# A two-layer streaming encoder step: the recurrence's projections and operands in one stage, the first tile's expert choice beside the second tile's chunks

## The chip, the cores and the metric

The kernel runs on one core of a Trainium2 chip. The number that counts is the time on the device in microseconds (us), as the median of three runs of the whole program. All data are float32. The engines are named PE (TensorE, matrix products), DVE (VectorE), ACT (ScalarE), POOL (GpSimd) and SP (SyncE, which only issues DMAs here).

## What is computed

384 tokens of width 1024 go through two layers: 256 of a prompt and 8 streams of 16 samples. Layer 0 mixes with an RWKV-7 recurrence, layer 1 with differential attention. Behind each mixer stands a PEER layer, which chooses 16 of 16384 experts per head (8 heads) and token:

```python
r, k, v = xr @ w_rkv[0], xk @ w_rkv[1], xv @ w_rkv[2]      # x* = x + (x_prev - x) * mu[i]
decay = exp(-exp(-softplus(-(w0 + tanh(xw @ w1) @ w2)) - 0.5)); a = sigmoid(a0 + (xa @ a1) @ a2)
S = S * d - (S kk)(kk * a)^T + v k^T;  y = S r             # token by token, 16 heads of 64
out = ((group_norm(y) + bonus) * g) @ w_out
x = layer_norm(ALPHA * x + out)
q = x @ w_query;  s = q . sub_keys                         # 2 x 128 scores a head
experts, gate = top 16 of the 16 x 16 sums of the best of each half, softmax
x = layer_norm(ALPHA * x + sum_k gate_k * gelu(u[e_k] . x) * v[e_k])
```

Each token and layer needs 128 rows of `u` and as many of `v`, 4 KB each. The kernel finds `u` and `v` of an expert side by side (8 KB).

## The kernel before

The tokens are three tiles of 128: tiles 0 and 1 are the prompt, tile 2 the samples. A stage is one block of the program with its own queues for each engine, and all engines meet at its end.

**Front part, one stage after the other.** `rwkv_projections` (L182) makes r, k, v, the decay's argument z, a and g of all three tiles and stores them in DRAM (`spill`). Then for tile 0 and again for tile 1: `wkv_operands` (L366; products of r, k, a with decays and their inverses), `wkv_chunks` (L465; the recurrence inside chunks of 16 tokens, 16 heads in groups of four), `wkv_states` (L787; the chunks' states in series) and `wkv_outputs` (L889; norm, own term, gate). Both tiles together: `load_rows` (L876), `to_features` (L939), `project_and_norm` (L990). After `mixing_weight` (L2342) and one more `to_features`, `open_flow` (L1523) makes the queries of both tiles and the scores and the choice of tile 0, and issues the first gathers.

**The flow.** `Flow` (L1175) spreads the experts' work over the stages that follow. One gather (`DMA_INDIRECT`, L1361) brings the `u` and `v` rows of one slot for 128 partitions, 1.05 MB; it is called a pair here, and there are 768, 128 for each tile and layer. A pair lands in one of 8 or 10 places of SBUF (`fl_pairs`, 8, and `fl_more`, 2 that are not there for the pairs in `NARROW`). DVE makes the dots with `u` (L1287), ACT the gelu (L1313) and the diagonal matrices (L1307), PE the sums with `v` (L1334), after which the place is free for the next gather. Two pairs are a unit, so there are 384. Each stage calls `flow.plan(ticks, last)` (L1224): it has `ticks` points at which a bit of the flow's work stands in each engine's queue, and `last` is the unit whose dots are due at its end. `turn_rows_out` and `turn_rows_in` (L1365, L1371) send a finished choice through DRAM into the order of the gathers. `Choice` (L1095) is the top-16 search on DVE, in small steps that also go into ticks.

**Beside the flow.** `mixing_tile` (L2963) does tile 2 of layer 0: for each half of the heads `half_operands` (L2393), `half_chunks` (L2510, 8 heads in groups of two, 35 ticks) and `half_outputs` (L2833), then the projection (`project_tile`, L2239) and the scores (`key_scores`). `attention_tile` (L3003) does layer 1 of a tile, three times. `run_flow` and `ffn_norm` end the program. Weights come in pieces of 1 MB through a ring of four places (`Pieces`, L1390, `pc_ring`).

Engines take their instructions in order; each queue waits by itself. POOL's queue holds the gathers, the products that spread operands over chunks (L776, L2816) and a few stores; SP's holds the weights' loads.

## Time and profile before

| | before |
|---|---|
| median of 3 runs | 3212.89 us (3206.84 to 3549.92) |
| span of the profiled execution | 3201.7 us |
| PE, PE weight loads | 66%, 35% busy |
| DVE, ACT, POOL | 56%, 21%, 33% busy |
| DMA | 1019.44 MB, mean 318 GB/s |
| HBM | 992.71 MB read, 18.39 MB written |

The profile is one execution. Its page cuts the span in 40 slices, 80 us each, with a digit for the busy share in tenths; further views give groups of instructions, waits, DMA issues and stretches. A stretch is written start:end in us from the span's start. In a group's line, x is the number of instructions, then busy us and the mean ns of one, then the engine's idle time before them and what ended most of it. The shares above are means over parts with different limits.

### The profile page before, as it was taken

The numbers are of one execution on the slowest core, as the hardware profiler recorded it, in microseconds if no ns is written. First come the engines' busy times: TensorE is split into PE (matmuls) and PEld (weight loads), VectorE is DVE, ScalarE is ACT, GpSimd is POOL, SyncE is SP. The second block draws the span as 40 slices with busy tenths as digits, with TensorE's granted clock in tenths as the row PEclk, the third lists the DMA queues.
The fourth block names the chain that finished last, engine by engine and source line by source line (L and its number), as shares of the span: only waits on it lengthen the run. The fifth ranks groups of instructions, "written<-read, shape, count | busy, mean of one in ns | idle before, by whom it ended". The sixth has DMA issues, their size and how long they took to land. (4 is left out here: it accounts for less than half of the span.)

```text
span 3201.7 us, 31542 instructions
## 1 busy us (share of the span) xinstructions
PE 2122.0 (66%) x10729; PEld 1110.6 (35%) x10729; DVE 1808.7 (56%) x4190; ACT 675.9 (21%) x1920; POOL 1060.0 (33%) x990
## 2 busy tenths in 40 slices
PE   6949668482577586758567585576767758655555
PEld 3427456270144253423224232234223434322222
DVE  2044454227786675576665765756744454965555
ACT  1012121010221321211431112511213221121111
POOL 0003122003356463334333333433333223454442
PEclk9979789795689797879788787788878878878877
DMA  5230200344889999999999999899999999999998
GB/s 173 92 138 1 78 3 18 110 130 199 346 324 369 372 389 408 420 404 403 408 371 420 399 397 416 345 413 420 383 412 405 420 401 410 360 383 421 420 420 335
DMA packets 152814, 1019.44 MB, mean 318 GB/s; under 512 B 17872, under 2 KB 18944, under 8 KB 37456
## 3 DMA queue, kind: packets, MB, share of 16 engines
q0 software_dynamic: 117024, 825.84, 64.2%
q1 hardware_dynamic: 35632, 191.58, 15.4%
q8 instruction: 88, 1.44, 0.2%
q14 instruction: 70, 0.57, 0.0%
HBM read 992.71 MB, written 18.39 MB: 316 GB/s over the span
## 5 line engine op out<-in xcount | busy, mean ns | idle before, releaser
L1334 PE MATMUL fl_acc<-fl_pairs,fl_diag 128*64 128x512 f32 x2576 | 820.8, 740 | 462.9 <-ACT fl_diag L1307 431.8
L1361 POOL DMA_INDIRECT fl_pairs<-in_peer_uv,fl_row_at x644 | 733.4, 1139 | 1116.0 <-PE fl_acc L1334 999.7
L1287 DVE CUSTOM_DVE_ANT_0 fl_pairs<-fl_pairs,fl_rows 128x1024 f32<-128x1024 f32 x644 | 789.5, 1245 | 398.3 <-DMA fl_pairs<-in_peer_uv,fl_row_at 396.9
L1334 PEld LDWEIGHTS fl_acc<-fl_pairs,fl_diag 128*64 128x64 f32 x2576 | 281.8, 162 | 879.4 <-issue 816.3
L1313 ACT ACTIVATE fl_acts<-fl_dots 128x2 f32<-128x2 f32 x384 | 78.0, 203 | 1247.6 <-DVE fl_dots L1287 1247.1
L1307 ACT ACTIVATE fl_diag<-constants_sb,fl_mix 128x64 f32<-128x64 f32 x768 | 224.2, 341 | 323.6 <-DVE fl_mix L1277 320.1
L1334 PE MATMUL fl_acc<-fl_more,fl_diag 128*64 128x512 f32 x496 | 171.7, 790 | 132.3 <-ACT fl_diag L1307 115.9
L1361 POOL DMA_INDIRECT fl_more<-in_peer_uv,fl_row_at x124 | 143.0, 1153 | 266.8 <-PE fl_acc L1334 245.9
L1287 DVE CUSTOM_DVE_ANT_0 fl_more<-fl_more,fl_rows 128x1024 f32<-128x1024 f32 x124 | 150.0, 1223 | 118.5 <-DMA fl_more<-in_peer_uv,fl_row_at 118.0
L1792 PE MATMUL aacc<-pc_ring,at_xT 128*128 128x512 f32 x288 | 139.8, 629 | 16.0 <-PEq L1719 16.0
L1334 PEld LDWEIGHTS fl_acc<-fl_more,fl_diag 128*64 128x64 f32 x496 | 60.1, 168 | 214.7 <-issue 206.0
L284 PE MATMUL acc<-w_ring,mixed 128*128 128x512 f32 x288 | 126.0, 599 | 10.0 <-issue 9.1
L1277 DVE TENSOR_TENSOR fl_mix<-fl_row_gate,fl_acts 128x2 f32<-128x2 f32 x384 | 68.8, 181 | 110.4 <-ACT fl_acts L1313 62.6
L1484 PEld LDWEIGHTS lbank_late<-at_yT,pc_ring 128*128 128x128 f32 x768 | 90.8, 197 | 25.3 <-issue 25.3
L1484 PE MATMUL lbank_late<-at_yT,pc_ring 128*128 128x128 f32 x768 | 95.9, 284 | 4.3 <-PEq L1719 4.3
L348 DVE SCALAR_TENSOR_TENSOR mixed<-dxT,mu_cols,xT 128x384 f32<-128x384 f32 x48 | 25.8, 612 | 114.5 <-PEq L293 114.5
L1792 PEld LDWEIGHTS aacc<-pc_ring,at_xT 128*128 128x128 f32 x288 | 54.1, 198 | 100.8 <-issue 100.8
L284 PEld LDWEIGHTS acc<-w_ring,mixed 128*128 128x128 f32 x288 | 55.1, 192 | 80.2 <-issue 80.2
L1579 PE MATMUL obank<-peer_xT,fl_pairs 128*128 128x256 f32 x256 | 58.2, 389 | 12.4 <-DMA fl_pairs<-in_query_by_head 12.4
L721 DVE TENSOR_TENSOR x<-bank,x 128x512 f32<-128x512 f32 x32 | 22.1, 692 | 75.1 <-PE bank L579 75.1
L1287 DVE DVE_READ_ACCUMULATOR2_ANT fl_dots<- 128x1 f32 x768 | 63.1, 82 | 0.0
L2052 PE MATMUL sa_b<-pc_ring,sa_pT 128*32 128x128 f32 x512 | 53.3, 299 | 13.8 <-ACT sa_pT L2082 13.8
(510 smaller groups left out, 2828.0 us busy)
## 6 DMA issues: line engine op xcount, KB each, us to landing
pc_ring<-in_kvq_by_pair SPq DMA_DIRECT2D x36, 1024.0 KB, 9.3
pc_ring<-in_query_by_head SPq DMA_DIRECT2D x32, 1024.0 KB, 9.8
pc_ring<-in_past_k SPq DMA_DIRECT2D x16, 1024.0 KB, 12.0
pc_ring<-in_past_v SPq DMA_DIRECT2D x16, 1024.0 KB, 11.2
w_ring<-in_rwkv_w_rkv SPq DMA_DIRECT2D x24, 512.0 KB, 3.6
pc_ring<-in_out_by_pair SPq DMA_DIRECT2D x12, 1024.0 KB, 9.8
fl_pairs<-in_peer_uv,fl_row_at POOLq DMA_INDIRECT x644, 16.3
fl_pairs<-in_query_by_head SPq DMA_DIRECT2D x8, 1024.0 KB, 11.0
```

What stands on the lines that cost most here:

```text
L284: mm = pe.matmul(acc[:, 2 * t + h, :], xm[:, k, t * P:(t + 1) * P], w_ring[:, n % RING, h * HALF:(h + 1) * HALF], start=(k == 0), stop=(k ...
L348: ins = dve.scalar_tensor_tensor(mixed[:, j % 2, k, :], dxT[:, k, :], mu_cols[:, i * KD + k:i * KD + k + 1], xT[:, k, 0:TOK], ALU.mult, AL ...
L1277: dve.tensor_tensor(self.mix[:, u % 2, q, :], self.row_gate[:, u % TILES, :, q], self.acts[:, u % 2, q, :], ALU.mult).then_inc(*self.mix_d ...
L1287: dve.tensor_tensor_reduce(pair, pair, self.rows[:, u % 2, j, :], 1.0, 0.0, ALU.mult, ALU.add, self.dots[:, u % 2, q, j:j + 1]).then_inc(* ...
L1307: act.activation(self.diag[:, self.diagged % self.DIAGS, j, :], self.core.const("fold_ident"), ACT.Copy, scale=self.mix[:, u % 2, q, j:j + ...
L1313: act.activation(self.acts[:, u % 2, q, :], self.dots[:, u % 2, q, :], ACT.Gelu).then_inc(*self.gelu_done.by())
L1334: mm = pe.matmul(self.acc[j * FOLD:(j + 1) * FOLD, half, :], self.diag[:, self.summed % self.DIAGS, j, :], self.pair(g)[:, D + half * HALF ...
L1361: pool.indirect_dma_start(self.pair(g), None, self.io["peer_uv"], bass.IndirectOffsetOnAxis(ap=self.row_at[:, u % TILES, j, q:q + 1], axis ...
L1484: mm = pe.matmul(self.bank[m % 3][:, 0:P], w[:, k, (m % 2) * P:(m % 2 + 1) * P], self.xT[:, k, :], start=(k == 0), stop=(k == KD - 1))
L1579: mm = pe.matmul(bank[m % 3][:, 0:WIDTH], wq[:, m // 2 % RING, k, (m % 2) * P:(m % 2 + 1) * P], xT[:, k, :], start=(k == 0), stop=(k == KD ...
L1792: mm = pe.matmul(acc[:, 2 * i + h, :], xT[:, k, :], pieces.tile(first + n // 2)[:, n % 2 * D + h * HALF:n % 2 * D + (h + 1) * HALF], start ...
L2052: mm = pe.matmul(o_bank[rows, g * P:(g + 1) * P], pT[:, g, j, rows], v, start=(j == 0), stop=(j == KT), tile_position=(0, h * HR))
```

## The change

**One stage for projections and operands.** `rwkv_operands` takes the place of `rwkv_projections` and of the operands' stages (`wkv_operands`, and `half_operands` for tile 2). The order of the six projections is now w, a, r, k, v, g, tile by tile within r, k, v, with the sums of the logs of the decay between them (`log_sums`). DVE makes the operands of a tile in two steps (`keys`, `decayed`), with one buffer for `e_incl`, `e_end`, `B`, `B_end`, `K_end` that the tiles share. POOL stores eight operands a tile in DRAM (`operands`, 4.2 MB a tile), and the own term and the gate (`gates`). Later stages load them into an `Operands` buffer.

**Order.** Then come `wkv_chunks` and `wkv_states` of tile 0. `Flow` and its accumulator are opened, and `half_chunks` runs over all 16 heads of tile 1 (`WideTile`, in groups of two: 63 ticks) with `FirstTile` in its ticks: outputs, projection, norm, queries, scores and choice of tile 0, with a ring of its own of two places for the 12 pieces of weights. Its gathers begin at the end of that stage. The ring of pairs is opened then (`open_ring`), and tile 1's states and outputs (`half_outputs`) follow, in which no pair is due before the states are done (`since`). `mixing_weight` stands after it with three ticks. `second_tile` does tile 1's projection, queries and scores beside the flow, with its own load of the same 12 pieces. Tile 1's choice moves into tile 2's chunks.

**Numbers.** `NARROW`, the pairs that have 8 places, is 0 to 195 (before 24 to 175), and all `last` numbers are new. The rest of the program is as it was.

```diff
-def rwkv_projections(core, io, buf):
...
+class Operands:
...
+    NAMES = ("a", "r", "B", "k", "v", "e_end", "B_end", "K_end")
...
+    def load(self, sp, t, parts):
+        for i, part in enumerate(parts):
+            for q in range(2):
+                sp.dma_start(self.tile[:, i, 4 * q:4 * q + 4], self.core.operands[t, :, part, 4 * q:4 * q + 4]).then_inc(*self.came[i][q].by(16))
+        self.since = [[s.last() for s in pair] for pair in self.came]
...
+def rwkv_operands(core, io):
...
+                def operands(t):
+                    for i, (n, src) in enumerate((("r", r[:, t]), ("B", B[:]), ("k", k[:, t % 2]), ("B_end", B_end[:]), ("K_end", K_end[:]), ("a", a[:, t]))):
+                        pool.wait_ge(*out_done.at(6 * t + i + 1))
+                        put(n, t, src, away[f"k{t % 2}" if n == "k" else n])
+                    put("e_end", t, e_end, away["e_end"])
...
+                lora("w")
+                lora("a")
+                project("r", 0)
+                log_sums(0, 0)
+                project("r", 1)
+                log_sums(0, 1)
+                project("r", 2)
+                project("k", 0)
+                project("k", 1)
+                log_sums(1, 0)
+                project("k", 2)
+                log_sums(1, 1)
+                project("v", 0)
+                log_sums(2, 0)
+                project("v", 1)
+                log_sums(2, 1)
+                project("v", 2)
+                lora("g")
...
+                        act.wait_ge(*away["e_end"].at(16 * t))
...
+                mix("w")
+                mix("a")
+                mix("r")
+                mix("k")
+                exclude(0, 0)
+                exclude(0, 1)
+                mix("v")
+                keys(0)
+                decayed(0)
+                exclude(1, 0)
+                keys(1)
+                exclude(1, 1)
+                mix("g")
+                decayed(1)
+                exclude(2, 0)
+                own_term(0)
+                keys(2)
+                own_term(1)
+                exclude(2, 1)
+                decayed(2)
+                own_term(2)
         core.end_stage()
...
-def wkv_operands(core, io, buf, w, t):
-def load_rows(core, io, gated, tiles):
-def wkv_outputs(core, io, buf, w, t):
-def to_features(core, src, dst, name, tiles):
-def project_and_norm(core, io, actT, weight, layer, name, tiles):
-def open_flow(core, io, flow, xT, last):
-def half_operands(core, io, flow, x, last, **events):
...
-    NARROW = range(24, 176)
+    NARROW = range(0, 196)
...
-            due = self.first + (self.last - self.first) * n // self.ticks
+            due = self.first + (self.last - self.first) * max(0, n - since) // (self.ticks - since)
...
+    def open_ring(self, ctx):
+        def sb(name, shape):
+            return ctx.enter_context(self.core.nc.sbuf_tensor("fl_" + name, shape, F32, side="right"))
+        self.ring, self.rows = sb("pairs", [P, self.KEPT, 2 * D]), sb("rows", [P, 2, GROUPS, D])
...
-    flow.plan(TICKS, last, lags=flow.LOOSE, **events)
+    beside.plan(TICKS, last, lags=Flow.LOOSE, **events)
...
+class FirstTile:
...
+    PLACES = 2
+    PIECES = KD // 2 + PH
...
+        for i in range(self.PIECES):
+            if i == self.PLACES:
+                sp.wait_ge(*self.vec_free.at(1))
+                sp.dma_start(self.vec[:, 0], io["ln_mix_g"][0:1, :].broadcast_to([P, D])).then_inc(*self.vec_in.by(16))
+                sp.dma_start(self.vec[:, 1], io["ln_mix_b"][0:1, :].broadcast_to([P, D])).then_inc(*self.vec_in.by(16))
+            if i >= self.PLACES:
+                sp.wait_ge(*self.used.at(i - self.PLACES + 1))
+            sp.dma_start(self.piece(i), sources[i]).then_inc(*self.came[i % self.PLACES].by(16))
+        sp.wait_ge(*self.rows_in.at(16 * TILES))
...
+            self.flow.turn_rows_out(pool, 0)
+            self.flow.turn_rows_in(pool, 0)
...
+        n = 30
+        for q in range(4):
+            yield n
+            dve.wait_ge(*self.s_done.at(q + 1))
+            part = choice.best_of(dve, choice.scores, q)
+            for i in range(4):
+                advance(part, 6)
+                n += 1
+                if i < 3:
+                    yield n
+            drain(part)
+        part = choice.rest(dve, 0)
+        while n < self.ticks:
+            yield n
+            advance(part, 4)
+            n += 1
+        yield n
+        drain(part)
...
+        for m in range(2 * PH):
+            yield 23 + m
...
+def second_tile(core, io, flow, x, gated, ops, at):
...
+            x = HalfTile(core, of_half, t, ops)
+            for part in range(2):
...
+        rwkv_operands(core, io)
...
+                    wkv_chunks(core, Operands(core, raw, "0", 2), w, 0)
+                ops = Operands(core, first, "1", 2, side="right")
+                wkv_states(core, w, 0, lambda sp: ops.load(sp, 1, range(2)))
+            flow = Flow(core, io, ctx)
+            first_gated = ExitStack()
+            rows = first_gated.enter_context(nc.sbuf_tensor("st_gated", [P, D], F32))
+            kept = ExitStack()
+            x = WideTile(core, kept, 1, ops)
+            with ExitStack() as beside:
+                half_chunks(core, FirstTile(core, io, flow, beside, both, carry, x), x)
+        flow.open_ring(ctx)
+        half_outputs(core, io, flow, x, rows, 6, since=NCH + 2, rows=((0, 1),))
+        kept.close()
+        mixing_weight(core, io, flow, neg_lam, 7)
+        with ExitStack() as of_sample:
+            ops = Operands(core, of_sample, "2", 1, side="right")
+            second_tile(core, io, flow, x, rows, ops, [(9, {}), (17, {}), (19, {}), (33, dict(rows=((1, 1),)))])
+            first_gated.close()
...
-    pieces = mixing_tile(core, io, flow, 2, None, later, [
-        (19, dict(choose=1, side=25)), (39, dict(side=50, end=18, turn=((1, 21, 24),))), (47, {}), (52, {}), (72, {}), (80, {}), (81, {}), (87, {}), (88, {}), (100, {})])
+    pieces = mixing_tile(core, io, flow, 2, ops, of_sample, later, [
+        (56, dict(choose=1, side=175, end=12, turn=((1, 15, 18),))), (64, {}), (82, {}), (90, {}), (92, {}), (99, {}), (101, {}), (110, {})])
```

## Rows read from the trace of the kernel before

**Rows 1.** The page's 40 slices of 80 us: DMA engines' busy share in tenths.
```profile
DMA  5230200344889999999999999899999999999998
```
**Rows 2.** Stretches (start:end, length, then as the first line says).
```profile
core 0: us, PE busy (x) PEld busy (x) DVE busy (x) ACT busy (x) POOL busy (x), PEclk, DMA share, GB/s
0.00:201.00 201.00, 166.78 (x405) 74.44 (x405) 38.36 (x72) 21.95 (x37) 11.43 (x20) 0.99 0.41 137
201.00:238.70 37.70, 5.35 (x8) 2.08 (x8) 22.60 (x21) 8.81 (x9) 0.00 (x0) 0.59 0.34 125
238.70:347.30 108.60, 95.76 (x656) 72.31 (x656) 44.31 (x89) 26.70 (x56) 42.61 (x45) 0.96 0.00 1
347.30:368.30 21.00, 19.61 (x512) 18.93 (x512) 8.40 (x19) 0.04 (x1) 0.00 (x0) 0.81 0.01 3
368.30:760.10 391.80, 228.13 (x1612) 173.00 (x1610) 170.35 (x392) 59.26 (x112) 50.30 (x59) 0.77 0.21 70
552.50:570.90 18.40, 2.12 (x13) 1.54 (x11) 12.31 (x13) 2.67 (x4) 0.00 (x0) 0.50 0.25 86
570.90:627.70 56.80, 33.94 (x80) 16.29 (x80) 14.05 (x22) 1.89 (x6) 0.00 (x0) 0.77 0.36 138
636.90:760.10 123.20, 65.27 (x322) 57.27 (x320) 54.30 (x210) 12.51 (x27) 7.72 (x14) 0.78 0.32 89
886.10:1005.60 119.50, 96.64 (x712) 57.69 (x712) 98.89 (x182) 31.39 (x102) 79.94 (x71) 0.93 0.86 334
1091.30:1199.80 108.50, 91.14 (x712) 55.71 (x712) 78.85 (x147) 30.58 (x104) 70.14 (x66) 0.97 0.99 388
1254.60:1391.70 137.10, 101.58 (x496) 55.75 (x496) 77.55 (x245) 26.04 (x91) 47.66 (x42) 0.85 1.01 419
1391.70:2822.70 1431.00, 968.51 (x4220) 453.87 (x4220) 890.77 (x2195) 346.91 (x1037) 503.99 (x463) 0.82 0.99 398
1005.60:3184.20 2178.60, 1446.55 (x6680) 688.00 (x6680) 1327.14 (x3120) 498.78 (x1531) 828.77 (x753) 0.82 0.99 401
```
**Rows 3.** DMA in 1005.6:3184.2: issues with KB each and median us to landing.
```profile
DMA packets 124870, 872.89 MB, mean 401 GB/s; under 512 B 14667, under 2 KB 15179, under 8 KB 21195
...
pc_ring<-in_past_k SPq DMA_DIRECT2D x16, 1024.0 KB, 12.0
...
fl_pairs<-in_peer_uv,fl_row_at POOLq DMA_INDIRECT x566, 17.0
...
fl_more<-in_peer_uv,fl_row_at POOLq DMA_INDIRECT x120, 17.3
```
**Rows 4.** Waits of DVE in 1005.6:3184.2: us in total, times, longest us.
```profile
DVE fl_pairs L1287 <- DMA fl_pairs<-in_peer_uv,fl_row_at: 369.7, 248, 4.3
```
**Rows 5.** Timeline of POOL, 744:762: start us, us, instruction, idle before and releaser.
```profile
753.15 0.59 POOL L1368 DMA_DIRECT2D turn_at<-fl_expert  x1 [110.58 <-DVEq L1172]
...
760.13 1.05 POOL L1361 DMA_INDIRECT fl_pairs<-in_peer_uv,fl_row_at  x1 [1.89 <-DMA fl_row_gate<-turn_gate]
```
**Rows 6.** The page's groups: PE's products of the projections.
```profile
L284 PE MATMUL acc<-w_ring,mixed 128*128 128x512 f32 x288 | 126.0, 599 | 10.0 <-issue 9.1
```
**Rows 7.** DMA issues over the whole span: KB each, median us to landing.
```profile
w_ring<-in_rwkv_w_rkv SPq DMA_DIRECT2D x24, 512.0 KB, 3.6
...
spill_v<-buf_v POOLq DMA_DIRECT2D x1, 1536.0 KB, 5.7
```
**Rows 8.** Groups by form, 886.1:1005.6, the first chunks' stage beside the pairs.
```profile
L1334 PE MATMUL fl_acc<-fl_pairs,fl_diag 128*64 128x512 f32 x160 | 44.3, 665 | 3.0 <-ACT fl_diag L1307 3.0
...
L2816 POOL TENSOR_TENSOR hc_B_by_chunk<-hw_B_end,constants_sb 128x512 f32<-128x512 f32 x8 | 10.4, 1304 | 0.1
```
**Rows 9.** Groups by form, 238.7:347.3, tile 0's chunks.
```profile
L776 POOL TENSOR_TENSOR v_by_chunk<-wkv_v,constants_sb 128x512 f32<-128x512 f32 x16 | 16.6, 1040 | 0.0
```
**Rows 10.** Groups by form, 1254.6:1391.7: queries of a tile and its projection.
```profile
L1484 PE MATMUL lbank_late<-mt_xT,pc_ring 128*128 128x128 f32 x256 | 32.9, 288 | 3.2 <-PEq L1719 3.2
...
L2276 PE MATMUL pt_acc<-pc_ring,mt_T 128*128 128x512 f32 x32 | 14.8, 604 | 3.2 <-PEq L1719 3.2
```

1376 lines of the change are left out of this document (669 added, 707 removed).

## Prediction

> **What bounds the kernel now.** I read the page's slices first [rows 1]. Read the DMA line: it stands at 9 from about the fifteenth slice to the end, and is low before that. So the kernel has a front part in which the DMA engines are mostly idle, and a long rest in which they are full. The table of stretches makes this exact [rows 2]: from 1005.6 us to 3184.2 us the DMA share is 0.99, at 401 GB/s, while PE is busy 1446.6 of 2178.6 us and DVE 1327.1. No compute engine is the limit there. What moves is the gathered pairs: 566 and 120 gathers of 128 rows of 8 KB, 1.049 MB each, are 719.3 MB of the 872.9 MB of this stretch [rows 3]. The waits of DVE in it agree: its longest ones are for pairs to land [rows 4]. The last 17.5 us hold the closing norm and no transfers that count.
>
> Ahead of the rest, the first gather is issued only at 760.1 us, 7.0 us after the first tile's choice is softmaxed [rows 5]. The stretch 368.3 to 760.1 runs at 70 GB/s: the second tile's operands, chunks, states and outputs, then both tiles' projection, then both tiles' queries, then the first tile's choice, one after the other. So two quantities decide the time: when the DMA engines become full, and how many bytes are left then.
>
> **The change, part by part.**
>
> *Projections and operands in one stage.* Before: 201.0 us, then 37.7 us of operands for tile 0 [rows 2], again 42 us for tile 1 (in the merged stretch), and two stages of them for tile 2 beside the pairs. After: one stage. PE keeps its 166.8 us and gets 12 sums of logs, 512 columns each, two passes apiece; the projections' row has 288 such passes in 126.0 us, 0.44 us each [rows 6], so 0.9 us for a sum and 10 us in all. DVE gets the operands of three tiles: 22.6 us each [rows 2], 68 us, beside 38.4 us it had. They hang in a chain with single buffers (`e_incl`, `e_end`, `B_end` are reused by each tile, and ACT waits for the last tile's DMA before it overwrites): a tile's keys and decays take some 21 us of DVE, then the store must land, some 6 us by the nearest row, 5.7 us for a store of 1.5 MB [rows 7], and PE's third tile waits on `log_sums`. PE's three projections take 45 us each with the sums, so the chain fits in except for two stalls of about 3 us. Then g's copies wait for the last operands, and the stage ends 6 us after the last store as before: 201 + 10 + 6 = 217 us. Bounds: 211 (no stall) and 201 + 68 = 269 (nothing hidden).
>
> *Chunks and states of tile 0.* Their code is the same: 108.6 and 21.0 us [rows 2]. The chunks now begin with loads of 1 MB pieces: PE waits for the first, some 6 us (512 KB took 3.6, 1 MB in a full queue 12.0 [rows 3, 7]). The operands' 37.7 us are gone. 217 + 114.6 + 21 = 353 us, against 368.3 before.
>
> *Tile 1's chunks (16 heads in groups of two, 63 ticks) with tile 0's outputs, projection, norm, queries and choice beside them.* This is the term that weighs most. PE: a stage of this code for 8 heads has PE busy 96.6 us, of which 44.3 are the pairs' products [rows 2, 8]; 52.3 remain, 105 for 16 heads. Beside it FirstTile has 14.8 us for the projection, 32.9 us for the queries [rows 10], and for the scores (32 passes, an eighth of the queries' 256) and the transposes some 8: 56 us. Together 161. DVE: 44.3 us for 16 heads by the nearest row, plus 12.3 us of outputs, 7 of norm (14.05 for two tiles) and 54.3 of choice [rows 2]: 118 us. In the two stages of this kind that the trace has, PE is busy 96.6/119.5 = 0.81 and 91.1/108.5 = 0.84 of the time, with DVE at 0.83 and 0.73 [rows 2]. With PE at 0.84 and less DVE I take 161/0.855 = 188 us, then 8 us for the exponent, the softmax and the turn of the rows (7.0 in [rows 5]). 353 + 196 = 549 us for the first gather, 211 us earlier. Bounds of the 188: 161 (PE never waits), and every inserted piece in series with the chain: 63 ticks at 119.5/35 = 3.4 us, 215 us, and 56 + 74 + 10 = 140 us on top, 355. The two-place ring of pieces is covered if a tick takes over about 3 us: a 1 MB piece serves two ticks and takes between 3.6 us (512 KB) and 12.0 us (1 MB, queue full) [rows 3, 7]; the queue is empty here, so I take it at the low end.
>
> GpSimd's spreading of the operands is also in this stage: 32 products and 8 diagonals. The row shows 1304 ns for one beside the pairs' two-input products on DVE, and 1040 ns in the stage without them [rows 8, 9]. The Trainium skill (GPSIMD Engine Reference, section Specifications) states that GpSimd shares its SBUF interfaces with VectorE and contends with it when DVE reads two SBUF inputs. The rows agree in direction, and the new stage puts more such DVE work beside it. At 1304 ns this is 52 us of GpSimd in a stage of 188, off the path, so both readings leave the sum where it is unless the chunks wait for it (a few us).
>
> *No pair handled until the second tile's states are done.* Gathers fill 8 places at once (8.4 MB, some 21 us), then the queue is idle. In the outputs' stage, the nearest rows are states 21.0 and outputs 18.4 us [rows 2]; six steps of dots stand among them, and the first sums come two ticks after the first dots. I take 48 us until a place comes free: full from 597 us, with 8 gathers issued. Bounds: 30 and 60.
>
> *What is left to move.* Before, 686 gathers were left at 1005.6 us [rows 3]; after, 760 are left at 597 us: 74 x 1.049 = 77.6 MB more. To this come tile 1's own 12 pieces, 12.6 MB (new: tile 1 no longer shares the projection and the queries with tile 0), tile 2's operands, 4.2 MB, against 2.1 MB of old ones, and 2.5 MB of norm vectors, rows and gates. 872.9 + 94.8 = 967.7 MB. At the 400.6 GB/s of this stretch that is 2416 us. So the change pays 31 us for the sharing given up, and this is in the sum.
>
> *The new schedule (`last` numbers) and tile 2.* Its first chunks now carry 23 units (two pairs each) instead of 20, and tile 1's whole final choice. That stage before was not full: 0.86 and 334 GB/s, DVE at 0.83 [rows 2]. With about 20 us more DVE work it would take some 140 us for 49 MB, which at 400.6 need 122: between 0 and 20 us lost, I take 10. Two operand stages are gone from there, which only takes work off engines that had time. Fewer places (8 to pair 195, not 175) cost nothing by the rows: the stretch 1091.3 to 1199.8 had 8 places and was full, 0.99 [rows 2]. The final part is as before.
>
> **Sum.** 597 + 2416 + 10 + 17.5 = 3040 us for the span, against 3201.7. The median shown, 3212.9, is 11 us over that span, so I predict 3051 us, 5.0% less. Range of this case alone: the merged stage from 161 to 230 us, the rate from 398 to 408 GB/s (398 was held over 1431 us [rows 2]): 2980 to 3115.
>
> **The rivals.**
>
> *Full rate, not average (chance 0.08).* If the new schedule keeps the queue as full as 1254.6 to 1391.7, 419 GB/s [rows 2], the rest takes 2310 us: 2945. Against it: the dips lie in attention and head norms, which are unchanged.
>
> *The merged stage turns into a chain (0.10).* PE, DVE and ACT take their queues in order, so each piece of FirstTile stands in the way of the chunk's next step. In [rows 2] that stage reaches PE 0.81 with the pairs beside it, which speaks against it; but its dots had no dependents among the chunks' neighbours, and FirstTile is itself one chain. At 260 to 355 us the time is 3123 to 3218.
>
> *Early part not full (0.08).* With 8 places and dense ticks, the part up to unit 110 (about 272 MB) could run at the 334 GB/s of 886.1 to 1005.6: 814 instead of 679 us, 3186 in all. The later stage of this kind, at 388 and 0.99 [rows 2], speaks against it. Here a rule of the skill would be harsher: DMA: Bandwidth & Descriptors, section Bandwidth, says that for transfers between HBM and SBUF the HBM side, some 358 GB/s, binds. By it the 967.7 MB would need 2703 us, and the kernel would be slower. The row shows 401 over 2178.6 us, so the measurement decides, and the rule has no part in the chance.
>
> *Slower (0.03).* The place: the merged stage's ring of two pieces. If it is a chain (355 us) and each of its 12 pieces is also waited for at 12.0 us, the longest landing row [rows 3], 144 us come on top: 499 us, 3362 in all. It decides from 415 us on: there the time passes 3277. Against it: this queue is empty while PE works, so pieces land sooner.
>
> *It does not do what it says (0.01).* If the first gather did not move, the time would be as before. Nothing in the diff suggests it; the stages that stood ahead of it are gone.
>
> **Chances.** The forecast has 0.70. A difference of 2% is about what a measurement of this kernel can tell from none, so the marks are 3149 and 3277. Faster: 0.70, plus 0.08, plus 0.07 of the chain (short of 3149) and 0.03 of the part not full: 0.88. Same: 0.03 + 0.05 + 0.01 = 0.09. Slower: 0.03. The range 2970 to 3120 holds most of the forecast's case and some of its neighbours, near 8 in 10.
>
> **What would show it.** The first gather near 549 us (before 760), the merged stage near 196 us with PE busy about 161, the first stage near 217, the DMA line at 9 from about 600 us on, some 968 MB after it at 400 GB/s. The prediction is wrong if the merged stage passes 260 us, if the DMA share between 600 and 1250 us stays under 0.9, or if the first stage is over 240 us because the reused buffers wait for their stores.

## Result, and the profile after

| | before | after |
|---|---|---|
| median | 3209.9 us | 3126.6 us (3121.8 to 3131.1) |
| ratio to before, 95% interval | | 0.976 [0.974, 0.979] |
| span of the profiled execution | 3201.7 us | 3128.9 us |
| DMA | 1019.4 MB, 318 GB/s | 1039.6 MB, 332 GB/s |
| PE, DVE busy | 66%, 56% | 69%, 57% |

The change gains 2.4%. (One run of the kernel before, 3549.9 us, was in a slower state of the chip; it stands in the median before and is left out of the ratio.) Forecast were 3051 us, 5.0%, and a range of 2970 to 3120, which the result misses by 6.6 us. The direction is as forecast, and the front part within 23 us; the gain is half the size.

The page's DMA line after the change, in 40 slices of 78 us, against [rows 1]:

```profile
DMA  3440330489979999989999999999999999889998
```

The full part begins at the ninth slice instead of the eleventh to thirteenth. But a 7 and several 8s stand in it. The table of stretches has the stages one by one (columns as in [rows 2]):

```profile
0.00:227.90 227.90, 179.22 (x429) 79.73 (x429) 96.83 (x123) 52.38 (x81) 29.34 (x48) 0.96 0.42 151
227.90:343.10 115.20, 98.63 (x656) 74.98 (x656) 43.26 (x88) 26.77 (x56) 42.69 (x45) 0.91 0.09 37
343.10:364.50 21.40, 19.53 (x512) 18.47 (x512) 8.40 (x19) 0.00 (x0) 0.00 (x0) 0.85 0.50 199
364.50:560.80 196.30, 161.44 (x1451) 132.90 (x1449) 114.04 (x322) 39.13 (x97) 46.01 (x49) 0.89 0.26 90
565.40:639.80 74.40, 37.99 (x536) 32.80 (x536) 31.61 (x47) 8.22 (x18) 14.54 (x18) 0.52 0.60 217
832.20:976.30 144.10, 107.44 (x736) 63.55 (x736) 120.77 (x240) 34.22 (x112) 82.59 (x77) 0.86 0.86 337
1035.30:1136.00 100.70, 87.91 (x655) 53.98 (x657) 71.98 (x131) 27.03 (x92) 64.34 (x60) 0.96 0.91 349
1367.10:1398.50 31.40, 12.82 (x32) 5.05 (x32) 29.04 (x55) 3.10 (x13) 5.79 (x5) 0.63 0.72 297
1814.70:1908.90 94.20, 75.57 (x200) 27.90 (x200) 53.04 (x98) 17.17 (x51) 35.67 (x32) 0.90 0.96 385
2351.40:2569.40 218.00, 155.77 (x1218) 90.76 (x1216) 104.14 (x263) 62.70 (x179) 59.98 (x56) 0.82 0.98 403
2695.20:2755.60 60.40, 30.75 (x80) 12.11 (x76) 57.46 (x131) 9.99 (x30) 23.10 (x22) 0.65 0.76 281
645.40:3111.10 2465.70, 1659.79 (x7837) 813.16 (x7833) 1488.81 (x3533) 540.36 (x1689) 940.53 (x858) 0.82 0.97 390
```

In the order of the rows: first stage; tile 0's chunks; its states; the merged stage; tile 1's states and outputs with the first gathers; tile 2's first and second chunks; the short stage with choice 2; one of the three attention projections; the sample attention; the stage of the last choice; all of it from the 13th gather on. For the like stages of the kernel before, beside [rows 2], four more rows of its table: the short stage with choice 2, attention projections, sample attention, last choice:

```profile
1420.40:1441.70 21.30, 10.15 (x29) 3.77 (x25) 16.44 (x58) 2.63 (x11) 8.71 (x8) 0.70 1.01 421
1441.70:1533.70 92.00, 72.54 (x200) 26.86 (x200) 53.19 (x98) 16.37 (x50) 38.66 (x32) 0.93 1.00 405
2748.60:2822.70 74.10, 43.11 (x120) 17.88 (x120) 68.28 (x155) 14.41 (x47) 34.58 (x32) 0.75 0.95 361
2381.80:2616.20 234.40, 156.91 (x1241) 89.92 (x1240) 111.52 (x278) 65.33 (x188) 67.61 (x62) 0.81 1.01 414
```

The fullest stretches stand at 419 to 421 GB/s, before and after. So I call *idle time* of a stretch its length times (1 - rate/420). The sample attention before: 234.4 x (1 - 414/420) = 3.3 us; the last choice after: 60.4 x (1 - 281/420) = 20.0 us. (The Trainium skill, Perfetto Trace Analysis, section Roofline, puts the ceiling of a core that works alone at its 16 DMA engines, about 435 GB/s; the rows agree with that and not with the 358 GB/s that the prediction weighed.)

The forecast's sum against the measured one, in us of span:

| term | forecast | measured | miss |
|---|---|---|---|
| first stage | 217 | 227.9 | +11 |
| tile 0's chunks and states | 136 | 136.6 | +1 |
| merged stage | 188 | 196.3 | +8 |
| to the first gather | 8 | 11.1 | +3 |
| from the first to the 13th gather | 48 + 4.2 MB at 400.6 = 58.5 | 73.5 | +15 |
| the rest | 963.5 MB at 400.6, + 10 = 2415 | 960.9 MB at 389.7: 2465.7 | +51 |
| the end | 17.5 | 17.8 | 0 |
| span | 3040 | 3128.9 | +89 |

The bytes are right within 2.6 MB (6 us), so the rate alone is 57 us too long. Its idle time is 2465.7 - 960.9/0.42 = 178 us; at 400.6 GB/s and with the 10 us it would be 121. Most of these 57 us stand in the stages above. Idle time after against the like stage before: tile 2's first chunks 28.5 against 5.6 at the average rate plus the 10 allowed (+13), its second chunks 17.0 against 8.3 (+9), the short stage 9.2 against 0 (+9), three attention projections 18.9 against 11.2 together (+8), sample attention 8.8 against 3.3 (+5), last choice 20.0 against 10.4 (+10): 54 us. These are six places picked because they lost; elsewhere gains and losses nearly cancel, such as 4 us less in the two prompt attentions and 5 us more in the norm behind the last choice.

### The profile page after: what moved, and what is told of

The parts are those of the page before. It is cut to its first block and busy times, and to the rows that moved or that the text cites. A ratio compares the mean times of both kernels' runs of the same rounds, so it can differ in the third digit from the quotient of the medians.

```text
span 3128.9 us, 33004 instructions
## 1 busy us (share of the span) xinstructions
PE 2164.7 (69%) x11433; PEld 1155.5 (37%) x11433; DVE 1792.7 (57%) x4150; ACT 672.7 (21%) x1953; POOL 1075.8 (34%) x1022
## 5 line engine op out<-in xcount | busy, mean ns | idle before, releaser
L1326 PE MATMUL fl_acc<-fl_pairs,fl_diag 128*64 128x512 f32 x2608 | 843.4, 751 | 463.4 <-ACT fl_diag L1299 431.9
L1684 PE MATMUL aacc<-pc_piece,at_xT 128*128 128x512 f32 x288 | 140.3, 632 | 12.3 <-PEq L1611 12.3
L367 PE MATMUL ro_acc<-ro_w_ring,ro_mixed 128*128 128x512 f32 x288 | 125.1, 593 | 0.5 <-PE ro_acc L367 0.5
L1479 PEld LDWEIGHTS lbank_late<-at_yT,pc_piece 128*128 128x128 f32 x768 | 91.9, 199 | 26.2 <-issue 26.2
L1479 PE MATMUL lbank_late<-at_yT,pc_piece 128*128 128x128 f32 x768 | 96.7, 285 | 4.5 <-PEq L1611 4.5
L1684 PEld LDWEIGHTS aacc<-pc_piece,at_xT 128*128 128x128 f32 x288 | 54.7, 201 | 100.0 <-issue 100.0
L367 PEld LDWEIGHTS ro_acc<-ro_w_ring,ro_mixed 128*128 128x128 f32 x288 | 54.9, 191 | 70.2 <-issue 70.2
L1944 PE MATMUL sa_b<-pc_piece,sa_pT 128*32 128x128 f32 x512 | 60.3, 324 | 26.0 <-ACT sa_pT L1974 26.0
L1944 PEld LDWEIGHTS sa_b<-pc_piece,sa_pT 128*32 128x32 f32 x512 | 53.3, 129 | 38.7 <-ACT sa_pT L1974 35.2
L1305 ACT ACT_TABLE_LOAD x47 | 60.3, 1283 | 0.8
L2168 PE MATMUL pt_acc<-pc_piece,at_oT 128*128 128x512 f32 x96 | 48.6, 644 | 8.6 <-PEq L2084 8.6
```

The source lines that it names most:

```text
L367: mm = pe.matmul(acc[:, 2 * t + h, :], mixed[:, j % 2, i, t * P:(t + 1) * P], w_ring[:, n % RING, cols[h]], start=(i == 0), stop=(i == KD ...
L1305: act.activation(self.acts[:, u % 2, q, :], self.dots[:, u % 2, q, :], ACT.Gelu).then_inc(*self.gelu_done.by())
L1326: mm = pe.matmul(self.acc[j * FOLD:(j + 1) * FOLD, half, :], self.diag[:, self.summed % self.DIAGS, j, :], self.pair(g)[:, D + half * HALF ...
L1479: mm = pe.matmul(self.bank[m % 3][:, 0:P], w[:, k, (m % 2) * P:(m % 2 + 1) * P], self.xT[:, k, :], start=(k == 0), stop=(k == KD - 1))
L1684: mm = pe.matmul(acc[:, 2 * i + h, :], xT[:, k, :], pieces.tile(first + n // 2)[:, n % 2 * D + h * HALF:n % 2 * D + (h + 1) * HALF], start ...
L1944: mm = pe.matmul(o_bank[rows, g * P:(g + 1) * P], pT[:, g, j, rows], v, start=(j == 0), stop=(j == KT), tile_position=(0, h * HR))
```

## Experiments

Times are medians, the ratio is to the kernel before with its 95% interval. A run's median can be off by a few us, so a small effect is read from the stage in which it stands. A stage also scatters: tile 2's first chunks, with the same schedule, take 141 to 144 us in the traces of nine kernels.

| run | us | ratio |
|---|---|---|
| e0_after | 3126.1 | 0.9758 [0.9741, 0.9775] |
| e1_since0 | 3115.6 | 0.9730 [0.9706, 0.9755] |
| e2_spread | 3119.4 | 0.9742 [0.9723, 0.9761] |
| e3_shift | 3137.7 | 0.9801 [0.9775, 0.9827] |
| e4_fewer_bytes | 3111.1 | 0.9712 [0.9696, 0.9729] |
| e5_two_e_end | 3111.3 | 0.9704 [0.9685, 0.9722] |
| e6_early_turn | 3149.7 | 0.9826 [0.9804, 0.9849] |
| e7_last_choice | 3119.9 | 0.9741 [0.9720, 0.9761] |
| e8_combo | 3070.8 | 0.9593 [0.9571, 0.9615] |
| e9_eight_places | 3199.5 | 0.9985 [0.9973, 0.9998] |
| e10_late_turn | 3117.3 | 0.9728 [0.9710, 0.9747] |
| e11_more_in_chunks | 3121.6 | 0.9755 [0.9729, 0.9780] |
| e12_combo_late | 3057.4 | 0.9565 [0.9531, 0.9599] |
| e13_combo_boundary | 3055.1 | 0.9558 [0.9524, 0.9592] |

**The changed kernel again (e0).**

> The changed kernel once more, beside the three runs that follow, as their common reference. Ratio to the kernel before 0.976, as recorded, within 0.003.

As expected. The others are compared with 3126 us. Below, a due number is a `last` number of the plan.

**Why the first stage takes 228 us (e5).** ACT's and PE's waits in the changed kernel's first stage (us, times, longest):

```profile
ACT L436 <- DMA operands<-ro_rows: 21.8, 1, 21.8
...
ACT ro_rows L436 <- DMA operands<-ro_rows: 13.9, 1, 13.9
```

```profile
PE ro_aux L385 <- DVE ro_z L512: 10.2, 1, 10.2
```

ACT may not write the next tile's `e_end` into the buffer from which POOL's store still reads. The edit (the first of its three places is the second buffer; that ACT writes and DVE reads them in turn is left out here):

```diff
+        e_ends = [rows[:, 2], sb("e_end2", [P, D])[:]]
...
-                        act.wait_ge(*away["e_end"].at(16 * t))
+                        if t == 2:
+                            act.wait_ge(*away["e_end0"].at(16))
```

> One buffer more for e_end in the first stage, so that ACT doesn't wait for the store of the tile before (waits of 13.9 and 21.8 us on it in the changed kernel; PE waits 10.2 us on z and 9.3 us on mixed behind them). Theory A (the stores' landing in the shared buffers is what makes this stage 227.9 us instead of the forecast 217): the stage becomes 8 to 12 us shorter, and the whole as much. Rival B (PE's waits come from DVE's queue, which does each tile's operands in order, and from the stores at the end): the stage is the same within 3 us.

The stage of e5:

```profile
0.00:210.00 210.00, 177.26 (x429) 79.12 (x429) 96.91 (x123) 52.82 (x81) 29.41 (x48) 1.00 0.46 164
```

18 us shorter with the same work, and the wait on `z` is gone; PE's clock stays at 1.00 where it was 0.96. The whole gains 15 us. Theory A holds, and stronger than the 8 to 12 us that I had put. 210 us is less than the lower bound of the forecast, 211. The gain in front arrives at the end nearly whole.

**Why the queue fills late (e1).** POOL's gathers in the changed kernel:

```profile
571.91 1.03 POOL L1353 DMA_INDIRECT fl_pairs<-in_peer_uv,fl_row_at  x1 [3.49 <-DMA fl_row_gate<-turn_gate]
...
580.77 0.95 POOL L1353 DMA_INDIRECT fl_pairs<-in_peer_uv,fl_row_at  x1 [0.30 <-issue]
625.95 1.02 POOL L1353 DMA_INDIRECT fl_pairs<-in_peer_uv,fl_row_at  x1 [44.24 <-PE fl_acc L1326]
...
645.65 0.94 POOL L1353 DMA_INDIRECT fl_pairs<-in_peer_uv,fl_row_at  x1 [14.61 <-PE fl_acc L1326]
```

Eight gathers, then nothing for 44 us, four more, and nothing for 15. The release is a sum of PE's each time.

```diff
-        half_outputs(core, io, flow, x, rows, 6, since=NCH + 2, rows=((0, 1),))
+        half_outputs(core, io, flow, x, rows, 6, rows=((0, 1),))
```

> One number: in the stage of tile 1's states and outputs, the six units are spread over all ticks from the first one on, not over the ticks behind the states. In the changed kernel the queue issues 8 gathers from 571.9 us on, then none until 625.9, and moves 217 GB/s in 565.4:639.8. Theory A (the places are the limit: the first sums come late, so nothing can be fetched): the ninth gather comes some 25 us earlier, the stage stays within 5 us of its 74.4 us, and the whole gains 10 to 20 us, 0.3 to 0.6%. Rival B (the states' chain is in series with whatever is put between its steps, so DVE's dots lengthen it by 12 x 1.2 us and PE's sums by some 10 us): the stage becomes 15 to 25 us longer, the bytes moved earlier are given back, and the whole is the same within 5 us.

```profile
562.70:629.80 67.10, 33.55 (x554) 25.45 (x556) 28.88 (x45) 8.06 (x20) 20.64 (x22) 0.65 0.82 304
```

The ninth gather comes 11 us behind the eighth. The stage is 5 to 7 us *shorter* (7 in these bounds, 5 from its first instruction to the next stage's): the states' chain leaves DVE and PE so idle (28.9 and 33.6 of 67.1 us busy) that the dots and sums lie in its gaps. Theory A holds. "No pair handled until the states are done" costs 10 us and protects nothing. Counted from the start of this stage, e1 is 16 us ahead of e0 where tile 2's chunks start, and 11 at the end, so some 5 us are lost again later.

**Tile 1's choice in tile 2's chunks (e2).** DVE's large operations of the choice in the changed kernel, start and us:

```profile
873.03 2.29 DVE L1137 TENSOR_TENSOR ch_scores<-constants_sb,ch_best 128x2048 f32<-128x2048 f32 x1
875.36 2.29 DVE L1139 TENSOR_TENSOR ch_scores<-ch_scores,ch_best_at_f 128x2048 f32<-128x2048 f32 x1
...
881.72 2.28 DVE L1140 TENSOR_REDUCE ch_found<-ch_scores 128x128 f32<-128x2048 f32 x1
884.03 2.29 DVE L1137 TENSOR_TENSOR ch_scores<-constants_sb,ch_best 128x2048 f32<-128x2048 f32 x1
886.36 2.29 DVE L1139 TENSOR_TENSOR ch_scores<-ch_scores,ch_best_at_f 128x2048 f32<-128x2048 f32 x1
888.68 2.29 DVE L1140 TENSOR_REDUCE ch_found<-ch_scores 128x128 f32<-128x2048 f32 x1
```

The choice is dealt out in steps, and a step may be 0.4 or 2.3 us. With five a tick (side 175 over 35 ticks) and a drain at tick 12, its dearest steps fall together, one unit's dots stand among them, and POOL issues no gather from 878 to 898 us.

```diff
-        (56, dict(choose=1, side=175, end=12, turn=((1, 15, 18),)))
+        (56, dict(choose=1, side=90, end=28, turn=((1, 30, 32),)))
```

> One schedule: in tile 2's first chunks, tile 1's choice is spread over 28 of 35 ticks (side 90, end 28, turn at 30 and 32), not over 12 (side 175, end 12, turn at 15 and 18). In the changed kernel this stage takes 144.1 us at 337 GB/s, with 20 us without a gather at 878 to 898, in which DVE runs six operations of 2.3 us of the choice nearly back to back. Theory A (the choice bunched in few ticks holds up the dots, so places come free late and the DMA queue runs dry): the hole at 880 to 900 goes, the stage takes 125 to 135 us, and the whole gains 10 to 18 us. Rival B (the stage is bound by DVE's sum, 120.8 us busy of 144.1, wherever the choice stands): the hole moves to another place, the stage stays at 140 to 146 us, and the whole is the same within 5 us.

```profile
832.90:965.20 132.30, 101.97 (x736) 60.66 (x736) 116.64 (x240) 34.12 (x112) 83.45 (x77) 0.93 0.92 362
```

12 us off the stage (9 against e0's trace, 141.4 us), idle time 18.3 us instead of 28.5; the whole gains 7 us by its median, where theory A said 10 to 18. Theory A in kind, for about a third of the stage's idle time.

**All due numbers lower by six (e3).**

```diff
-        (56, dict(choose=1, side=175, end=12, turn=((1, 15, 18),))), (64, {}), (82, {}), (90, {}), (92, {}), (99, {}), (101, {}), (110, {})])
+        (50, dict(choose=1, side=175, end=12, turn=((1, 15, 18),))), (58, {}), (76, {}), (84, {}), (86, {}), (93, {}), (95, {}), (104, {})])
```

and so on to 263, which becomes 257.

> All due numbers from tile 2's first chunks to the last attention tile's projections are 6 units lower (50 for 56, up to 257 for 263), so that the units move into the sample attention (34 instead of 28 due there). Theory A (the last 64 pairs' units wait for the last choice, so a lead gained in front leaves too few units for the last attention tile, where the queue then runs half empty: 54 us of idle queue from 2216 to 2786 us against 30 us before, counted against 420 GB/s; besides, gathers 384 and 512 wait 27 and 28 us for their choice): the idle there falls by 10 to 25 us, the chunks' stage shortens by 15 to 20 us, and the whole gains 10 to 25 us, 0.3 to 0.8%. Rival B (it is DMA bound all along and the order of the units makes no difference): the same within 6 us. Rival C (DVE and PE bound in the sample attention): the sample attention stage grows by 6 x 6 us or more and the whole is the same or slower.

```profile
828.30:951.90 123.60, 93.34 (x635) 57.37 (x637) 104.27 (x207) 28.55 (x91) 64.21 (x64) 0.85 0.78 296
1788.90:1880.40 91.50, 73.67 (x200) 26.91 (x200) 53.19 (x98) 16.38 (x50) 37.26 (x32) 0.91 1.00 406
2322.90:2572.80 249.90, 158.65 (x1264) 90.47 (x1264) 119.22 (x293) 67.47 (x198) 74.18 (x68) 0.81 0.98 402
```

12 us slower: theory A falls, and rival C comes nearest (it said 36 us more in the sample attention, and the same or slower). Six units less (17 instead of 23) took 19 to 20 us off the chunks' stage, some 3.2 us a unit, and raised its idle time to 36 us. Six more cost 32 us in the sample attention (5.3 us a unit; 2.1 MB at 400 GB/s are 5.2). The last choice's stage, with the same 10 units, takes 60.3 us as against 60.4. So a unit is cheap in a stage that DVE bounds and dear in one that the queue bounds. What did become better is the attention projection in which gather 384 falls: 3.0 us idle instead of 7.9.

**Units into the last choice's stage (e7).**

```diff
-        (291, {}), (294, {}), (298, {}), (300, {}), (306, {})])
+        (285, {}), (288, {}), (292, {}), (294, {}), (300, {})])
```

> Six units are moved from the sample attention into the stage of the last choice: due numbers 285, 288, 292, 294, 300 for 291, 294, 298, 300, 306. In the changed kernel that stage (14 ticks, choice 5) takes 60.4 us for 9.5 units at 281 GB/s with DVE busy 57.5 us; before it took 74.1 us for 15 units at 361 GB/s. Theory A (DVE sets this stage, so a unit costs only its 2.5 us of dots there, and 5.2 to 5.8 us of DMA elsewhere): the stage becomes 72 to 76 us long, the sample attention 30 to 35 us shorter, and the whole gains 10 to 18 us. Rival B (a unit costs the same wherever it stands): the same within 5 us.

```profile
2350.30:2536.00 185.70, 138.66 (x1176) 83.12 (x1176) 87.46 (x231) 58.73 (x162) 45.86 (x43) 0.87 0.99 406
2666.60:2753.70 87.10, 44.18 (x120) 18.25 (x120) 71.95 (x160) 14.72 (x49) 41.63 (x40) 0.72 0.96 371
```

These rows go from a stage's first instruction to the next one's; in the changed kernel the same two are 216.6 and 70.1 us (the last choice's, 60.4 in the table above, goes on for 10 us after its dots, with the engines waiting for the choice's rows). Six units (16 instead of 10) cost 17 us there, 2.8 each, and their leaving saved 31 us of sample attention, 5.2 each, as theory A has it. The norm of the heads between them grew by 3. So 11 us are gained where the last choice's stage ends (9 against e0's trace), but the whole gains 6 us where 10 to 18 were expected: theory A in kind, short in size.

**More units in tile 2's first chunks (e11).**

```diff
-        (56, dict(choose=1, side=175, end=12, turn=((1, 15, 18),))), (64, {}), (82, {}), (90, {}), (92, {}), (99, {}), (101, {}), (110, {})])
+        (60, dict(choose=1, side=175, end=12, turn=((1, 15, 18),))), (68, {}), (86, {}), (94, {}), (96, {}), (101, {}), (102, {}), (110, {})])
```

> Tile 2's first chunks carry 27 units instead of 23, and the four units are taken from the stages between 1207 and 1364 us (due numbers 60, 68, 86, 94, 96, 101, 102, 110). With 16 units (the run with all due numbers lower) that stage took 123.6 us, with 23 it takes 141 to 144: 2.7 us a unit. Theory A (the stage is bound by DVE and PE, so a unit there costs 2.7 us and in the full stages 5.0 us): it takes 152 to 156 us, the later stages 20 us less, and the whole gains 6 to 12 us. Rival B (with 8 places the sums can't be freed that fast, and the stage grows by 5 us a unit or more): the same or slower.

```profile
832.70:993.80 161.10, 117.98 (x768) 66.89 (x768) 130.20 (x260) 36.65 (x124) 94.87 (x85) 0.84 0.88 352
```

Four units cost 17 us here (4.3 each), and the stages behind it, up to the one with choice 2, gave back 19. The whole is 5 us less, within the interval: inconclusive. From 17 to 23 units one cost some 3.2 us, from 23 to 27 it cost 4.3.

**Choices 3 and 4 earlier (e6), choice 2 later (e10).** In the changed kernel, rows of POOL around gather 384:

```profile
1849.69 0.59 POOL L1361 DMA_DIRECT2D turn_gate<-fl_gate  x1
...
1870.49 1.31 POOL L1370 DMA_DIRECT2D fl_row_at<-turn_at  x2 [16.29 <-DMA turn_gate<-fl_gate]
...
1879.81 1.01 POOL L1353 DMA_INDIRECT fl_pairs<-in_peer_uv,fl_row_at  x1 [6.81 <-DMA fl_row_gate<-turn_gate]
```

The choice's way through DRAM (64 KB for each of its two tables) takes 30 us with the queue full, and POOL, in order, issues nothing while it waits.

```diff
-            (180, dict(rows=((3, 1),), choose=3, side=20)), (182, dict(side=20)), (196, dict(side=50, end=9, turn=((3, 11, 13),)))
+            (180, dict(rows=((3, 1),), choose=3, side=25)), (182, dict(side=35)), (196, dict(side=50, end=3, turn=((3, 5, 7),)))
```

> The choices 3 and 4 (layer 1 of tiles 0 and 1) get the numbers of choice 2: side 25 and 35 in the two short stages, end 3, turn at 5 and 7 in place of 20, 20, end 9, turn at 11 and 13. In the changed kernel gathers 384 and 512 are issued 27 and 28 us after the ones before them, released by the choice's rows. Theory A (the queue runs dry while the choice travels through DRAM): the two gaps fall under 15 us and the whole gains 8 to 16 us. Rival B (the choice's six operations of 2.3 us then fall into two or three ticks of a short stage and hold up the dots there, as at 1380 to 1398 in the changed kernel, where no gather is issued for 18 us with side 35): the loss moves there, and the whole is the same within 5 us.

```profile
1796.20:1824.60 28.40, 9.84 (x25) 4.12 (x25) 26.82 (x51) 2.43 (x10) 4.74 (x4) 0.56 0.76 309
2230.40:2256.40 26.00, 5.47 (x16) 2.44 (x17) 24.67 (x45) 1.70 (x7) 1.89 (x2) 0.57 0.68 284
```

The gaps before gathers 384 and 512 went (1.5 us before 384), but others came: 20 us before gather 372, 28 before 502. And the kernel became 23 us slower. The two rows are the second short stages of choices 3 and 4, again from first instruction to first instruction. They take 28.4 and 26.0 us in place of 18.5 and 14.0, with DVE busy for nearly all of it: 22 us more, nearly the whole loss. Rival B, and worse: the loss did not move, it was made. So the opposite edit was tried on choice 2, which the change had put in this way:

```diff
-            (114, dict(rows=((2, 1),), choose=2, side=25)), (117, dict(side=35)), (130, dict(side=50, end=3, turn=((2, 5, 7),))), (136, {}),
+            (114, dict(rows=((2, 1),), choose=2, side=20)), (117, dict(side=20)), (130, dict(side=50, end=9, turn=((2, 11, 13),))), (136, {}),
```

> Choice 2 (layer 0 of tile 2) gets the numbers that it had before the change: side 20 and 20 in the two short stages, end 9, turn at 11 and 13, for 25, 35, 3, 5 and 7. In the changed kernel the second short stage takes 29.9 us for 2.5 units, with 17 GB/s at 1390 to 1400; the like stages of the other two tiles take 14.9 and 9.9 us. Theory A (the choice in a short stage is DVE's alone and costs what it takes, some 14 us; a gather that waits for its choice costs less, as the 10 places cover 25 us of it): the stage shortens by 12 to 16 us, gather 256 comes up to 25 us after gather 255, and the whole gains 3 to 12 us. Rival B (both cost the same): the same within 3 us.

```profile
1369.10:1388.20 19.10, 11.16 (x33) 4.66 (x33) 15.53 (x52) 3.10 (x13) 5.58 (x6) 0.75 1.01 419
1388.20:1480.90 92.70, 74.05 (x202) 28.10 (x202) 51.84 (x95) 16.75 (x50) 38.40 (x33) 0.92 1.00 409
1390.00:1410.00 20.00, 19.02 (x54) 6.92 (x52) 19.86 (x22) 1.58 (x6) 10.99 (x7) 1.00 1.01 421
```

The short stage is 12 us shorter (19.1 us for 31.4) and full. POOL now issues nothing for 26 us, before gather 254 already, as it stands in its queue at the choice's return; still the stage behind idles 2.4 us, where it idled 3, for the 10 places cover most of the wait. The whole gains 9 us, as theory A expected.

The third row shows something that the theories don't have. The choice's six operations of 2.3 us now stand in the projections, from 1391.7 to 1407.7 us, as close together as before (1376.7 to 1393.1), and the queue stays full, at 421 GB/s. In the changed kernel's short stage it ran dry:

```profile
1390.00:1400.00 10.00, 5.33 (x11) 2.27 (x12) 7.87 (x15) 1.38 (x5) 1.55 (x2) 0.53 0.08 18
```

In e10 PE makes the sums of three units among the six operations (from 1392.2, 1397.7 and 1403.7 us), so places come free; in the short stage it makes none between 1379 and 1394. So falling together is not enough for a loss: in these traces it costs where few units are due among the steps.

**What sharing costs (e4).** Tile 1's own pieces are loaded only in part, so the kernel leaves out 7.9 MB of its query weights:

```diff
+            part = slice(0, P if self.name == "early" and n >= self.PLACES else 2 * D)
-            sp.dma_start(self.tile(n), self.sources[n])
+            sp.dma_start(self.tile(n)[:, part], self.sources[n][:, part])
```

> Of the 12 pieces of 1 MB that tile 1 now loads for itself, the last 8 (its query weights) are cut to their first 128 columns, so that 7.9 MB fewer are moved; the rest of each place keeps an older piece, and tile 1's queries, and all that follows from them, are not the reference's. Theory A (from 645 us on the DMA engines set the time, and bytes cost what they cost on average): 7.9 MB at 400 GB/s are 20 us, so the whole takes 16 to 22 us less than the changed kernel, and the 12.6 MB of sharing given up cost some 31 us. Rival B (the stages there are bound by PE and DVE beside the transfers): under 8 us less.

15 us for 7.9 MB, 1.9 us a MB, where the average rate says 2.5. The medians alone would leave 8 us of doubt, but the stretch with these loads, up to tile 2's chunks, is shorter by 15 us too (163.0 for 178.0). So the 12.6 MB of sharing given up cost about 24 us rather than 31, an estimate from this run.

**Eight places for all pairs (e9).**

```diff
-    NARROW = range(0, 196)
+    NARROW = range(0, 768)
```

> All pairs have 8 places, those from 196 on too, which have 10 in the changed kernel. Nothing else is changed. Theory A (places are what decides whether the queue stays full where the dots come in bursts: 16 MB in flight and in use instead of 20): the stages of attention lose 2 to 4 us each, and the whole is 25 to 60 us slower. Rival B, that of the forecast (8 places keep the queue full): the same within 8 us.

The stages of prompt attention, with 8 places:

```profile
1534.70:1614.10 79.40, 47.02 (x144) 16.43 (x144) 47.50 (x125) 39.52 (x99) 25.27 (x22) 0.65 0.81 314
1990.80:2074.70 83.90, 48.41 (x160) 18.44 (x160) 52.68 (x123) 42.09 (x98) 24.06 (x22) 0.71 0.79 299
```

and in the changed kernel:

```profile
1516.70:1581.10 64.40, 38.77 (x144) 14.04 (x140) 46.44 (x123) 39.18 (x98) 25.04 (x22) 0.79 0.97 389
1946.20:2013.70 67.50, 42.83 (x168) 16.91 (x167) 52.84 (x125) 41.74 (x98) 26.52 (x23) 0.85 0.93 374
```

Two places are worth 73 us, more than theory A's range, and nearly all that the change had gained. (A place holds 1.05 MB, so it is 8.4 MB in place of 10.5, not the 16 and 20 of the expectation.) My forecast had said that fewer places cost nothing, from one stage of chunks; in attention, where dots come in bursts, that is wrong by 15 us a stage, 31 of the 73 in the two. Ten places for the early pairs, where I had claimed it, weren't tried.

**Together (e8, e12, e13).** e8 is e1, e2, e5 and e7 in one kernel; e12 adds e10; e13 lowers the due numbers from 176 to 263 by four besides.

> Four single edits together: the units of tile 1's outputs spread over all ticks, tile 1's choice spread over 28 ticks, a second e_end buffer, six units moved to the stage of the last choice. Alone they gave 10.5, 7, 15 and 6 us against the changed kernel. Theory A (each removes idle time of the DMA queue at a place of its own, and the queue is the limit of all that follows): they add up, 35 to 40 us, the whole at 3086 to 3093 us, a ratio to the kernel before of 0.964. Rival B (idle time removed in front comes back later, at the choices that the flow then reaches earlier): 20 to 28 us.

By their ratios against e0's the single edits (e1, e2, e5, e7) gave 9, 5, 17 and 5 us, each within some 9 us, 37 together; the four together give 53. That is more than theory A's 35 to 40, and the sum of the single ones is itself uncertain by some 25 us. So they add up, rival B (20 to 28) falls, and whether they help each other stays open. Against the changed kernel's trace, the stage starts of e8 are early by 17 us after the first stage, 34 at tile 2's chunks, 46 behind them, and still 46 at the sample attention.

> The four edits together (3071 us) and choice 2 with its numbers of before, which alone gave 9 us. Theory A (idle time removed at one place is not given back later): 3060 to 3064 us. Rival B (the later choices' waits take it back): 3068 to 3072 us.

3057 us: theory A again, 4.4% below the kernel before. With the losses named here mended, the change comes near the 5.0% that I had forecast without them.

> As the run beside it, and from the end of attention tile 0 to tile 2's projections all due numbers are 4 lower, so that the flow reaches the first pairs of choices 3 and 4 (gathers 384 and 512, which wait 26 to 28 us) two ticks later; the four units go into the sample attention. With 6 units less the idle time of these two stages fell from 7.9 and 7.8 to 3.2 and 4.5 us, counted against 420 GB/s. Theory A (the rest of the idle time in attention comes from gathers that wait for a choice): both gaps under 20 us, 5 to 8 us less than the run beside it. Rival B (it comes from the order of dots and sums in the ticks, and the choice's trip is covered by the 10 places): the same within 3 us.

```profile
1733.20:1829.90 96.70, 73.42 (x200) 27.88 (x200) 53.32 (x98) 16.38 (x50) 37.33 (x32) 0.94 0.99 408
1867.20:1934.40 67.20, 40.72 (x160) 15.95 (x160) 52.13 (x123) 41.88 (x98) 25.23 (x22) 0.78 0.92 365
```

The gaps before gathers 384 and 512 are under 13 us, but POOL's wait for the choice only moved: it now issues nothing for 25 us before gather 376 and for 17 before 504. The two projections idle 2.8 and 3.3 us instead of 7.6 and 8.1 in e12. But the prompt attention behind the first now idles 8.8 us (6.2 in e12), and the whole is 2 us less, within the interval. The waits for choices 3 and 4 are worth little; rival B is nearer.

## Why the prediction was right, and where it was wrong

*What bounds it, and the bytes.* Right. 14.7 + 960.9 MB from the first gather on, 976.1 forecast. What is won in front arrives at the end: e5 won 18 us in the first stage and 15 in the whole. Of the forecast's signs of being wrong none clearly came, but one was close: the DMA share from 600 to 1250 us is 0.90, just at its mark.

*The first stage.* The step that failed is "the chain fits in except for two stalls of about 3 us". I saw the shared buffers and named them, but priced a stall by a store that has the queue to itself, 5.7 us [rows 7]. ACT waited 21.8 and 13.9 us. Part of that is the way to the store, which stands behind six others in POOL's queue, each of which waits for DVE: 8 us both times. The rest is its landing:

```profile
139.72 0.81 POOL L294 DMA_DIRECT2D operands<-ro_rows  x1
153.36 1.28 ACT L436 ACT_TABLE_LOAD   x1 [21.76 <-DMA operands<-ro_rows]
139.00:154.00 15.00, 7.42 (x18) 3.00 (x16) 0.00 (x0) 0.64 (x1) 1.38 (x2) 0.87 1.02 405
```

The first store took 13.6 us, with the other stores and the weights' loads in the same DMA engines (405 GB/s); the second, issued at 183.1 us, took 5.5, as [rows 7] has it. e5 shows the price of the shared buffer: 18 us.

*Chunks, states, merged stage.* Right: 136.6 for 136, and PE busy 161.4 us where 161 was summed. The merged stage took 196.3 for 188, PE at 0.82 of it instead of 0.855. The rival of a chain (260 us and more) did not come. GpSimd's products were hardly slowed in it:

```profile
L2566 POOL TENSOR_TENSOR hc_K_by_chunk_1w<-ops,constants_sb 128x512 f32<-128x512 f32 x16 | 17.7, 1107 | 0.0
L2566 POOL TENSOR_TENSOR hc_B_by_chunk_1w<-ops,constants_sb 128x512 f32<-128x512 f32 x16 | 16.7, 1042 | 0.8 <-PE hc_bank_1w L2380 0.8
```

These are groups of the merged stage: 1042 and 1107 ns, near the 1040 of [rows 9] and not the 1304 of [rows 8], though DVE does FirstTile's two-input products beside them. DVE is busy 0.58 of this stage, and 0.83 of [rows 8]'s, but that share doesn't decide it: in tile 2's first chunks of the changed kernel DVE is busy 0.84, and the same two groups take 1065 and 1059 ns. What made 1304 stays open.

*Until the queue is full.* The step "I take 48 us until a place comes free: full from 597" was mis-sized: 54 us to the ninth gather, and a second gap of 15 us that I hadn't seen. Only two units are summed in that stage, so only four places come free. I also took it for granted that this time was the price of the states; e1 shows that it need not be paid.

*The rate.* This is the term that made the forecast wrong: 57 of the 89 us. I carried an average of 400.6 GB/s over to a schedule in which the stages carry other numbers of units and the choices stand elsewhere, and allowed 10 us; the measured 389.7 lies below even the 398 of my range. For tile 2's first chunks my own figures had it (140 us for bytes that need 122, measured 144), and I took 10 of the 18. An average rate belongs to a schedule. What the runs showed in its place: choice steps that fall together on DVE where few units' sums stand among them (the first chunks, e2, 9 to 12 us of stage; the short stage, e10, 9 us; e6, the same made twice more, 23 us), a last choice's stage with too few units (e7, 6 us), and the order of ticks in attention, whose rest stays open. The sentence "the final part is as before" was the mistake in one line: its code is as before, its numbers aren't.

*The rival "early part not full"* (334 GB/s up to unit 110) was half right: tile 2's two chunk stages ran at 337 and 349, but 645.4 to 1364.2 us as a whole at 382.

*From span to median.* I added 11 us. In every run on record an execution's time is 2 to 3 us over its own span; the 11 came from comparing the median with the span of another execution. The changed kernel's median is 2 us under its profiled span, so this hid 13 us of the sum's miss.

*Open.* Of the 57 us, e2, e7 and e10 return 22 by their medians. The second chunks (9 us), the sample attention (5 us) and the projections (8 us) are located in the trace and not explained by a run.

## What to carry to other kernels

Where a queue is the limit, forecast the stretches in which it will not be full, stage by stage under the new schedule, and don't carry an average over. A piece of work that is dealt out in steps is best dealt out by duration, and its long steps kept out of short stages: six steps of 2.3 us that fell together left the queue dry for 10 us and more where few sums stood among them, and cost nothing where three did. In a chain of small dependent steps there is room for other work, so try it before keeping the two apart, and give a buffer whose store waits behind others a second copy.

## What the runs showed that I had not expected

Two more places of 1 MB in a ring of eight are worth 73 us of 3200 (e9), where one stage before had shown 8 places and a DMA share of 0.99. A choice takes 30 us through DRAM and back while the queue is full, though it is small, and POOL issues no gather for 17 to 28 us of it; yet the attention projections in which this falls idle only 2.4 to 7.9 us in all (e10, e13, the changed kernel). And moving steps of a choice by a few ticks changed the kernel by +23 and -9 us, the first as much as the 12.6 MB of weights that the change loads a second time (about 24 us).
